# Attention on one core: values times turned probabilities as three products of rounded parts, copied out of PSUM by two engines

## The chip, the cores and the metric

The kernel runs on 1 core of one Trainium2 chip. The metric is the device time of one execution in microseconds. The core has five engines that work beside each other: TensorE (PE in the profile, PEld for its weight loads), VectorE (DVE), ScalarE (ACT), GpSimd (POOL) and SyncE (SP, which starts the DMAs). They order their work by semaphores alone, and each takes its own instructions strictly in order. TensorE's results lie in PSUM, in banks of 512 float32 columns.

## The reference

One step of a two-layer backbone over 640 tokens of width 1024: 512 latent tokens and 128 context tokens. Layer 0 mixes tokens by attention, layer 1 by pooling; behind each comes a mixture of experts with product keys, which takes most of the time. The change lies in the attention:

```python
def block_attention(q, k, v):
    ...
    def one(qi):
        sc = jnp.einsum('bqkgd,btkd->bkgqt', qi, k).astype(jnp.float32) * scale
        p = jax.nn.softmax(sc, axis=-1).astype(v.dtype)
        return jnp.einsum('bkgqt,btkd->bqkgd', p, v)
```

There are 8 query heads and 2 key/value heads of 128. A latent query sees 640 keys (128 cached and 512 of its own), a context query the 128 context keys. All is float32.

## The kernel before

The work of all engines around the attention follows one list, `order_of_units` (L100). It is written out by hand, and TensorE (L1675) and ScalarE (L854) both walk it; VectorE's order is written out separately (`attention`, L1049). A unit of the list has a name and a class, and the class fixes the PSUM tensor: scores go to `bankA` in turns, turned probabilities to `bankD[0]` (class T), the products with the values and some modulation products to `bankD[1]` (class M). Each of these tensors spans two banks.

The stage has 8 heads with 5 tiles of 128 queries, so 40 scores, numbered n = 5 x head + tile. Tiles 0 to 3 are latent (640 keys), tile 4 is context (128 keys). For each n the list says: score n, for n mod 5 = 4 in the first six heads a modulation product (`ada`), for n mod 5 = 0 behind those heads its turned form (`adat`), for n mod 5 = 2 from n = 7 on the values product (`pv`) of the head before, and then the transposes (`pt`) of n-2.

- TensorE: `score` (L1771 to L1783) two matmuls of 512 and 128 columns, `pt` (L1784 to L1789) five transposes of 128x128, side by side in `bankD[0]`, columns 0 to 640; `pv` (L1790 to L1798) five float32 matmuls with 512 columns, the values `vA` against the turned probabilities `PT`, and one with 128 columns for the context tile. A float32 matmul has two records in the trace.
- ScalarE, in the list's order: the exponential of score n with its sum (L945; it waits for VectorE's maximum and for the transposes of n-2, L887 to L890), the copies of `ada` (L894) and `adat` (L897), and for `pv` the copy of the output (L948) and its rounding to float32r (L950). Behind head 6 it also rounds two blocks of the output weights (L951 to L954, through L837).
- VectorE, for each n (L1126 to L1134): `row_max(n)` (L1104, L1105), `normalise(n-1)` (L1111, L1112), `keep_transposed(n-2)` (L1115 to L1124), which copies `bankD[0]` to `PT` and frees the bank, and for n mod 5 = 4 from head 1 on the low part of the head before (`head_rest`, L1035).

`prob` has two buffers, `PT` two (L319, in the place of `sq`), `bankD[0]` one. Behind the stage stands the output projection `wo` (L1799 to L1816), which works with rounded parts already: a high part, rounded to float32r, and a low part, the rest, and three products of them (high x high, high x low, low x high). The expert stage does the same (L1594 to L1608). The parts of the normed input, `hhi` and `hlo`, serve the projections ahead of the stage only, and the last rows of `headr`/`headw` the rotary.

Of the kernel before, what the change touches and what calls it, by code (L numbers as in the profile page):

```python
# [18 lines left out]
ALU = mybir.AluOpType  # L19
# [5 lines left out]
P = 128  # L25
# [7 lines left out]
NH, NKV, HD = 8, 2, 128  # L33
KT = (P + TS) // P
SCALE = HD ** -0.5
EPS = 1e-6
# [159 lines left out]
def build(nc, ins, outs):  # L196
# [47 lines left out]
    with ExitStack() as ctx:  # L244
# [24 lines left out]
        gate = sb("gate", [P, NG])  # L269
        aval = sb("aval", [P, NG])  # L270
        actg = sb("actg", [P, NG])
# [9 lines left out]
        with ExitStack() as front:  # L281
# [36 lines left out]
            ow_split = [split_pair(headr, b) for b in range(2)]  # L318
            PT = sq[:, :, :].rearrange("p k t -> p (k t)").rearrange("p (b j q) -> p b j q", b=2, j=KT)  # L319
            with ExitStack() as rt:  # L320
# [88 lines left out]
        ohi_ready = sem("ohi_ready")  # L409
        olo_ready = sem("olo_ready")  # L410
        sq_ready = sem("sq_ready")
        scaled = sem("scaled")
# [305 lines left out]
        def _(act):  # L718
# [135 lines left out]
            for name, cls in ORDER:  # L854
# [4 lines left out]
                if kind == "wo" and name[1] < K - 2:  # L859
                    act.wait_ge(d_full, Dn[name] + 1)  # L860
                    split_weight(NSPLIT + name[1] + 2)
                if cls not in ("A", "M"):
                    continue
# [78 lines left out]
                elif kind == "score":  # L942
                    b = name[1] % 2
                    w = KT * P if name[1] % TILES < TILES - 1 else P
                    act.activation(prob[:, b, 0:w], bank[:, 0:w], ACT.Exp, bias=smx[:, b, 1:2],  # L945
                                   scale=of_unit(rq, name[1]), accum_out=smx[:, b, 2:3]).then_inc(a_free, 1)
                elif kind == "pv":
                    act.copy(OT[:, name[1], :], bank[:, 0:T]).then_inc(m_free, 1)  # L948
                    act.wait_ge(m_free, n + 1)
                    act.copy(ohi[:, name[1], :], OT[:, name[1], :]).then_inc(ohi_ready, 1)  # L950
                    if name[1] == NH - 2:  # L951
                        act.wait_ge(rope_done, NH + NKV)
                        split_weight(NSPLIT)
                        split_weight(NSPLIT + 1)  # L954

        @block.vector
        def _(v):
# [91 lines left out]
            def attention():  # L1049
# [65 lines left out]
                def keep_transposed(n):  # L1115
# [4 lines left out]
                    if t < TILES - 1:  # L1120
                        v.tensor_copy(PT[:, h % 2, :, t * P:(t + 1) * P],
                                      bankD[0][:, 0:KT * P].rearrange("p (j q) -> p j q", q=P)).then_inc(t_free, 1)
                    else:
                        v.tensor_copy(PTp[:, h % 2, :], bankD[0][:, 0:P]).then_inc(t_free, 1)  # L1124

                for n in range(NH * TILES + 2):  # L1126
                    if n < NH * TILES:
                        row_max(n)
                    if 1 <= n <= NH * TILES:
                        normalise(n - 1)  # L1130
# [328 lines left out]
        def _(pe):  # L1459
# [215 lines left out]
            for name, cls in ORDER:  # L1675
# [108 lines left out]
                elif kind == "pt":  # L1784
# [3 lines left out]
                    for j in range(KT if name[1] % TILES < TILES - 1 else 1):  # L1788
                        last = pe.transpose(bank[:, j * P:(j + 1) * P], prob[:, name[1] % 2, j * P:(j + 1) * P], ident)  # L1789
                elif kind == "pv":  # L1790
                    h = name[1]
                    kv = h // (NH // NKV)
                    pe.wait_ge(t_free, Tn[("pt", h * TILES + TILES - 1)] + 1)
                    pe.wait_ge(a_free, A[("v", TILES - 1)] + 1)
                    for j in range(KT):
                        pe.matmul(bank[:, 0:TS], vA[:, j, kv * HD:(kv + 1) * HD], PT[:, h % 2, j, :],
                                  start=j == 0, stop=j == KT - 1)
                    last = pe.matmul(bank[:, TS:T], vP[:, kv * HD:(kv + 1) * HD], PTp[:, h % 2, :], start=True, stop=True)  # L1798
# [114 lines left out]
```

## Time and profile before

| | |
|---|---|
| three runs, median | 3225.47 us (3223.08 to 3232.5) |
| the profiled execution, its span from the first to the last instruction | 3225.0 us |
| mean granted TensorE clock in it | 0.985 |
| busy: TensorE, VectorE, GpSimd, ScalarE | 3107.2, 2872.3, 1999.2, 1110.5 us |

For the profiled execution its span is the one time that is given. Busy times are sums over instructions; matmuls are pipelined and their ends modelled, so that records overlap and a busy TensorE is not one at its peak. The row of an instruction has its start, its length and, in brackets, how long its engine had stood idle before it and what ended that. "issue" is a wait that the profile can't name.

### The profile page before, as it was taken

What the parts mean: (1) busy time and instruction counts of PE and PEld (TensorE: products, weight loads), DVE (VectorE), ACT (ScalarE), POOL (GpSimd) and SP (SyncE); (2) the same over time, 40 slices, a digit from 0 to 9 for tenths busy, and PEclk for the clock granted to TensorE, in tenths of its full rate; (3) what the DMA queues carried; (4) which work ended last, traced back from release to release, by engine and by line L of the source; (5) the groups of instructions that cost most, each with busy time, mean ns of one, the idle gap of its engine ahead of it and who ended that gap; (6) DMA issues with size and microseconds to landing.
All of it is one profiled execution on the core that took longest, in us unless ns stands there. A gap on an engine that the chain in (4) does not pass through costs nothing.

```text
span 3225.0 us, 50321 instructions
## 1 busy us (share of the span) xinstructions
PE 3107.2 (96%) x15946; PEld 2595.0 (80%) x15946; DVE 2872.3 (89%) x5518; ACT 1110.5 (34%) x1693; POOL 1999.2 (62%) x1483
## 2 busy tenths in 40 slices
PE   7998999989999999999997999979999999999998
PEld 6857566669999999999986466669999999999997
DVE  3574699999999999999998699999999999999998
ACT  3332333333333333333333233333333333333333
POOL 1000166677778887777773067767777877777773
PEclk9999999999999999999998999989999999999999
DMA  5230456689999999999997354589999999999995
GB/s 241 78 135 28 157 215 254 256 346 409 408 408 399 407 399 389 410 408 401 376 406 283 151 196 195 222 314 409 405 409 401 403 404 387 410 408 404 401 400 226
DMA packets 248396, 1044.93 MB, mean 324 GB/s; under 512 B 23024, under 2 KB 72944, under 8 KB 205808
## 3 DMA queue, kind: packets, MB, share of 16 engines
q0 software_dynamic: 147456, 536.94, 42.2%
q1 hardware_dynamic: 100848, 506.86, 39.8%
q8 instruction: 47, 0.77, 0.1%
q14 instruction: 45, 0.37, 0.0%
HBM read 990.49 MB, written 53.22 MB: 324 GB/s over the span
## 4 chain that ended last, share of the span: by engine, by line
PE 77%; DVE 11%; issue 5%; DMA 4%; POOL 1%; ACT 1%; DVEq 1%; POOLq 0%; SPq 0%; ACTq 0%
PE bankA L1594 10%; PE bankA L1596 10%; PE bankA L1595 10%; PE bankD L1607 6%; PE bankD L1608 6%; PE bankD L1606 6%; PE bankA L1548 5%; PE bankA L1608 3%; PE bankA L1607 3%; PE bankA L1606 3%; PE bankD L1516 2%; DMA hT<-in_v,idxc 2%; DVE wch L1370 2%; DMA wch<-in_wq 2%; DVE hot L1320 2%
## 5 line engine op out<-in xcount | busy, mean ns | idle before, releaser
L1594 PE MATMUL bankA<-hh,uh 128*128 128x384 f32 x2048 | 689.4, 337 | 25.6 <-DVE ul L1354 25.6
L1596 PE MATMUL bankA<-hh,ul 128*128 128x384 f32 x2048 | 689.3, 337 | 0.0
L1595 PE MATMUL bankA<-hl,uh 128*128 128x384 f32 x2048 | 687.8, 336 | 0.0
L681 POOL DMA_INDIRECT hT<-in_v,idxc x320 | 469.2, 1466 | 161.5 <-issue 72.2
L681 POOL DMA_INDIRECT hT<-in_u,idxc x320 | 466.5, 1458 | 164.8 <-issue 75.4
L807 ACT ACTIVATE wt<-bankA 128x384 f32<-128x384 f32 x256 | 126.0, 492 | 1120.5 <-PE bankA L1596 881.7
L1594 PEld LDWEIGHTS bankA<-hh,uh 128*128 128x128 f32 x2048 | 386.2, 189 | 37.4 <-issue 26.6
L1370 DVE SCALAR_TENSOR_TENSOR wch<-hT,a,wch 128x1024 f32<-128x1024 f32 x320 | 399.5, 1280 | 10.6 <-DMA hT<-in_v,idxc 6.4
L1607 PE MATMUL bankD<-vl,wh 128*128 128x512 f32 x1024 | 399.9, 390 | 0.0
L1608 PE MATMUL bankD<-vh,wl 128*128 128x512 f32 x1024 | 399.4, 390 | 0.0
L1606 PE MATMUL bankD<-vh,wh 128*128 128x512 f32 x1024 | 398.3, 389 | 0.0
L1595 PEld LDWEIGHTS bankA<-hl,uh 128*128 128x128 f32 x2048 | 386.1, 189 | 9.8
L1361 DVE CUSTOM_DVE_ANT_0 hT<-hT,htok 128x1024 f32<-128x1024 f32 x320 | 382.6, 1221 | 11.7 <-DMA hT<-in_u,idxc 9.4
L647 POOL TENSOR_TENSOR mask<-mask,topf 128x1024 f32<-128x1024 f32 x36 | 84.1, 2358 | 494.9 <-DVE mask L1281 494.9
L1596 PEld LDWEIGHTS bankA<-hh,ul 128*128 128x128 f32 x2048 | 385.7, 188 | 0.0
L1382 DVE TENSOR_TENSOR vl<-vraw,vh 128x1024 fp32r<-128x1024 f32 x256 | 312.7, 1221 | 27.0 <-ACT vh L811 23.7
L681 POOL DMA_INDIRECT wch<-in_u,idxc x192 | 293.7, 1530 | 59.6 <-issue 59.6
L1354 DVE TENSOR_TENSOR ul<-uraw,uh 128x1024 fp32r<-128x1024 f32 x256 | 312.2, 1220 | 0.3
L1548 PE MATMUL bankA<-wch,hT 128*128 128x512 f32 x640 | 289.5, 595 | 3.3 <-DMA wch<-in_wq 1.9
L681 POOL DMA_INDIRECT wch<-in_v,idxc x192 | 232.1, 1209 | 63.3 <-issue 60.5
L797 ACT CAST uh<-uraw 128x1024 fp32r<-128x1024 f32 x256 | 268.8, 1051 | 0.0
L811 ACT CAST vh<-vraw 128x1024 fp32r<-128x1024 f32 x256 | 266.4, 1041 | 0.0
(244 smaller groups left out, 5632.9 us busy)
## 6 DMA issues: line engine op xcount, KB each, us to landing
uraw<-in_uT SPq DMA_DIRECT2D x128, 1024.0 KB
vraw<-in_vP SPq DMA_DIRECT2D x128, 1024.0 KB
wch<-in_wq SPq DMA_DIRECT2D x32, 2048.0 KB, 7.6
gates_scratch<-gbuf SPq DMA_DIRECT2D x12, 4096.0 KB, 11.8
wch<-gates_scratch SPq DMA_DIRECT2D x64, 768.0 KB
wch<-in_ada SPq DMA_DIRECT2D x19, 2048.0 KB, 7.5
wch<-in_qkv SPq DMA_DIRECT2D x3, 2048.0 KB, 23.9
adap<-in_ada SPq DMA_DIRECT2D x3, 2048.0 KB, 17.3
```

The source lines that it names most:

```text
L681: pool.indirect_dma_start(out=row_buf[slot], out_offset=None, in_=table.rearrange("l e d -> (l e) d"), in_offset=bass.IndirectOffsetOnAxis ...
L1354: v.tensor_tensor(ul[:, c, :], uraw[:, b, c * D:(c + 1) * D], uh[:, c, :].bitcast(F32), ALU.subtract).then_inc(ul_ready, 1)
L1361: v.tensor_tensor_reduce(out=row_buf[r % RING], in0=row_buf[r % RING], in1=htok[:, r % GT, :], scale=1.0, scalar=0.0, op0=ALU.mult, op1=AL ...
L1370: v.scalar_tensor_tensor(out=acc[:, r % GT, :], in0=row_buf[r % RING], scalar=a8[:, r:r + 1], in1=acc[:, r % GT, :], op0=ALU.mult, op1=ALU ...
L1382: v.tensor_tensor(vl[:, c % 2, :], vraw[:, b, c % 2 * D:(c % 2 + 1) * D], vh[:, c % 2, :].bitcast(F32), ALU.subtract).then_inc(vl_ready, 1)
L1548: last = pe.matmul(bank, hT[:, k, t * P:(t + 1) * P], w[:, k, :], start=k == 0, stop=k == K - 1)
L1594: pe.matmul(abank[c], hi, hh[:, k, :], start=k == 0, stop=False)
L1595: pe.matmul(abank[c], hi, hl[:, k, :], start=False, stop=False)
L1596: last = pe.matmul(abank[c], lo, hh[:, k, :], start=False, stop=k == K - 1)
L1606: pe.matmul(y, hi, vh[:, c, a:a + 512], start=first, stop=False)
L1607: pe.matmul(y, hi, vl[:, c, a:a + 512], start=False, stop=False)
L1608: last = pe.matmul(y, lo, vh[:, c, a:a + 512], start=False, stop=final)
```

## The change

The turned probabilities and the values are each split in a high part (rounded to float32r) and a low part, and the values product becomes three float32r products for each of the five key tiles: 15 matmuls with 512 columns in place of five float32 ones. ScalarE writes the high part of the turned probabilities from PSUM, VectorE subtracts it from PSUM to get the low part. The five transposes now go to columns 0 to 384 (one bank) and 512 to 768 (the other), and each bank has a copy and a subtraction of its own. The high parts of the values are written once by ScalarE ahead of the first exponential, the low parts by VectorE in step n = 2. The parts lie in tensors that are unused in this stage (`hhi`, `hlo`, the end of `headr`), and the last low part of the values takes the place of `aval`, which serves later.

```diff
+PTCUT = ((0, 3), (3, KT))
...
-        aval = sb("aval", [P, NG])
+        with ExitStack() as plain:
+            aval = sb("aval", [P, NG], where=plain)
+        vlast = sb("vlast", [P, NKV * HD], F32R)
...
-            PT = sq[:, :, :].rearrange("p k t -> p (k t)").rearrange("p (b j q) -> p b j q", b=2, j=KT)
+            parts_of = lambda x: x[:, :, :].rearrange("p k t -> p (k t)").rearrange("p (b j q) -> p b j q", b=2, j=KT)
+            PTh, PTl = parts_of(hhi), parts_of(hlo)
+            v0 = headr[:, 10 * T - (2 * KT - 1) * NKV * HD:10 * T].rearrange("p (j n) -> p j n", n=NKV * HD)
+            vhi, vlo = v0[:, 0:KT, :], v0[:, KT:2 * KT - 1, :]
...
+                if cls == "T" and name[1] % TILES < TILES - 1:
+                    h, t = divmod(name[1], TILES)
+                    if t == 0 and h >= 2:
+                        act.wait_ge(m_full, Mn[("pv", h - 2)] + 1)
+                    act.wait_ge(t_full, Tn[name] + 1)
+                    for i, (j0, j1) in enumerate(PTCUT):
+                        act.copy(PTh[:, h % 2, j0:j1, t * P:(t + 1) * P],
+                                 bankD[0][:, i * 512:i * 512 + (j1 - j0) * P].rearrange("p (j q) -> p j q", q=P)).then_inc(pth_ready, 1)
...
+                    if name[1] == 0:
+                        act.wait_ge(att_in, 48)
+                        act.wait_ge(a_free, A[("v", TILES - 1)] + 1)
+                        act.copy(vhi, vA[:, :, :]).then_inc(vhi_ready, 1)
                     act.activation(prob[:, b, 0:w], bank[:, 0:w], ACT.Exp, bias=smx[:, b, 1:2],
...
-                        v.tensor_copy(PT[:, h % 2, :, t * P:(t + 1) * P],
-                                      bankD[0][:, 0:KT * P].rearrange("p (j q) -> p j q", q=P)).then_inc(t_free, 1)
+                        for i, (j0, j1) in enumerate(PTCUT):
+                            v.wait_ge(pth_ready, (h * (TILES - 1) + t) * 2 + i + 1)
+                            some = PTh[:, h % 2, j0:j1, t * P:(t + 1) * P].bitcast(F32)
+                            last = v.tensor_tensor(PTl[:, h % 2, j0:j1, t * P:(t + 1) * P],
+                                                   bankD[0][:, i * 512:i * 512 + (j1 - j0) * P].rearrange("p (j q) -> p j q", q=P),
+                                                   some, ALU.subtract)
+                        last.then_inc(t_free, 1)
...
+                    if n == 2:
+                        v.wait_ge(vhi_ready, 1)
+                        v.tensor_tensor(vlo, vA[:, 0:KT - 1, :], vhi[:, 0:KT - 1, :].bitcast(F32), ALU.subtract)
+                        v.tensor_tensor(vlast[:, :], vA[:, KT - 1, :], vhi[:, KT - 1, :].bitcast(F32), ALU.subtract
+                                        ).then_inc(vlo_ready, 1)
...
-                        last = pe.transpose(bank[:, j * P:(j + 1) * P], prob[:, name[1] % 2, j * P:(j + 1) * P], ident)
+                        o = j * P if j < PTCUT[0][1] else 512 + (j - PTCUT[0][1]) * P
+                        last = pe.transpose(bank[:, o:o + P], prob[:, name[1] % 2, j * P:(j + 1) * P], ident)
...
+                    pe.wait_ge(vlo_ready, 1)
                     for j in range(KT):
-                        pe.matmul(bank[:, 0:TS], vA[:, j, kv * HD:(kv + 1) * HD], PT[:, h % 2, j, :],
-                                  start=j == 0, stop=j == KT - 1)
+                        cols = slice(kv * HD, (kv + 1) * HD)
+                        pe.matmul(bank[:, 0:TS], vhi[:, j, cols], PTh[:, h % 2, j, :], start=j == 0, stop=False)
+                        pe.matmul(bank[:, 0:TS], vhi[:, j, cols], PTl[:, h % 2, j, :], start=False, stop=False)
+                        rest = vlo[:, j, cols] if j < KT - 1 else vlast[:, cols]
+                        pe.matmul(bank[:, 0:TS], rest, PTh[:, h % 2, j, :], start=False, stop=j == KT - 1)
```

## Rows read from the trace of the kernel before

**Rows 1.** The page, busy time and its share of the span, by engine.

```profile
PE 3107.2 (96%) x15946; PEld 2595.0 (80%) x15946; DVE 2872.3 (89%) x5518; ACT 1110.5 (34%) x1693; POOL 1999.2 (62%) x1483
```

**Rows 2.** The table of stretches: stretch, length, busy time of each engine, granted clock.

```profile
144.40:279.55 135.15, 118.67 (x556) 67.68 (x556) 93.19 (x216) 50.60 (x110) 0.00 (x0) 0.96 0.27 103
```

**Rows 3.** The timeline of one head, VectorE (DVE), ScalarE (ACT): start us, length us, engine, line.

```profile
193.54 0.81 DVE L1104 TENSOR_REDUCE smx<-bankA 128x1 f32<-128x640 f32 x1
...
199.13 0.82 DVE L1121 COPY sq<-bankD 128x640 f32<-128x640 f32 x1 [3.86 <-PE bankD L1789]
...
199.99 0.68 ACT L948 COPY qT<-bankD 128x640 f32<-128x640 f32 x1
...
200.21 0.83 DVE L1104 TENSOR_REDUCE smx<-bankA 128x1 f32<-128x640 f32 x1 [0.26 <-PE bankA L1781]
...
200.70 0.73 ACT L950 CAST qTr<-qT 128x640 fp32r<-128x640 f32 x1
...
201.33 0.88 ACT L945 ACTIVATE prob<-bankA,smx,rq 128x640 f32<-128x640 f32 x1
...
202.59 0.28 DVE L1104 TENSOR_REDUCE smx<-bankA 128x1 f32<-128x128 f32 x1
...
203.63 0.46 ACT L945 ACTIVATE prob<-bankA,smx,rq 128x128 f32<-128x128 f32 x1 [1.33 <-DVE smx L1105]
...
204.08 0.57 ACT L894 COPY adar<-bankD 128x512 f32<-128x512 f32 x1
...
204.43 0.82 DVE L1035 TENSOR_TENSOR qTr<-qT,qTr 128x640 fp32r<-128x640 f32 x1
...
205.16 0.82 DVE L1104 TENSOR_REDUCE smx<-bankA 128x1 f32<-128x640 f32 x1
...
207.35 0.15 ACT L897 COPY mod<-bankD 128x8 f32<-128x8 f32 x1
...
207.57 0.82 DVE L1104 TENSOR_REDUCE smx<-bankA 128x1 f32<-128x640 f32 x1 [0.21 <-PE bankA L1781]
...
208.68 0.89 ACT L945 ACTIVATE prob<-bankA,smx,rq 128x640 f32<-128x640 f32 x1 [1.18 <-DVE smx L1105]
...
209.42 0.82 DVE L1104 TENSOR_REDUCE smx<-bankA 128x1 f32<-128x640 f32 x1
```

**Rows 4.** The same timeline, TensorE.

```profile
193.72 4.53 PE L1796 MATMUL bankD<-sq,vA 128*128 128x512 f32 x10 [0.76 <-issue]
...
198.31 0.71 PE L1789 MATMUL bankD<-const,prob 128*128 128x128 f32 x5
```

**Rows 5.** The timeline of the expert stage, TensorE.

```profile
1500.02 0.39 PE L1607 MATMUL bankD<-vl,wh 128*128 128x512 f32 x1
...
1500.70 0.39 PE L1607 MATMUL bankD<-vl,wh 128*128 128x512 f32 x1
```

**Rows 6.** Groups by line: duration ns min/median/max, first and last start us.

```profile
L1074 DVE TENSOR_TENSOR ropes<-bankD,trig x10: 684/692/693, 82.5 to 143.5; 128x512 f32<-128x512 f32 x10
...
L837 ACT CAST headr<-wch x8: 1040/1048/1049, 264.5 to 321.8; 128x1024 fp32r<-128x1024 f32 x8
```

**Rows 7.** The timeline, ScalarE ahead of the first exponential.

```profile
145.82 1.28 ACT L945 ACT_TABLE_LOAD   x1 [0.95 <-PE bankA L1781]
```

**Rows 8.** The timeline around three rests, and the clock of one microsecond.

```profile
250.37 0.77 PE L1789 MATMUL bankD<-const,prob 128*128 128x128 f32 x5 [1.73 <-DVE sq L1121]
...
256.93 4.53 PE L1796 MATMUL bankD<-sq,vA 128*128 128x512 f32 x10 [0.47 <-issue]
...
265.93 0.77 PE L1789 MATMUL bankD<-const,prob 128*128 128x128 f32 x5 [1.73 <-DVE sq L1121]
...
268.97 1.33 PE L1789 MATMUL bankD<-const,prob 128*128 128x128 f32 x5 [2.27 <-DVE sq L1121]
...
272.12 7.20 PE L1796 MATMUL bankD<-sq,vA 128*128 128x512 f32 x10 [0.43 <-issue]
...
267.00:268.00 1.00, 0.00 (x0) 0.63 0.00 0
```

More of the change, by code:

```diff
@@ L410, in build @@
         olo_ready = sem("olo_ready")
+        vhi_ready = sem("vhi_ready")
+        vlo_ready = sem("vlo_ready")
+        pth_ready = sem("pth_ready")
         sq_ready = sem("sq_ready")
```

## The prediction

> **What bounds the kernel now.** I read the page's busy line first: TensorE is busy 96% of the span, VectorE 89%, ScalarE 34% [rows 1]. That is an average over stages, and the edit touches one of them only: from 144.4 to 279.6 us, between the rotary and the output projection. The table of stretches gives that stage 135.15 us, with TensorE busy 118.7, VectorE 93.2 and ScalarE 50.6, so nobody is full [rows 2]. Everything behind the stage waits for it (the output projection needs the last head), and its loads wait for uses, so a delay here should pass to the end one for one.
>
> The order in time says what the limit is. The stage repeats once per head, 40 units in all, five to a head. I number them by n mod 5: units 0 to 3 are wide (640 keys), unit 4 is narrow (128). From one head's row maximum of unit 2 (193.54) to the next head's (209.42) 15.88 us pass [rows 3]. In it TensorE runs ten records for the values product, 4.5 us in one piece, and the next transposes start 4.59 us after it [rows 4]; meanwhile VectorE waits 3.86 us for those transposes, and so does ScalarE. In the rest of the head VectorE works without a stop: the starts of its row maxima follow each other by 2.38, 2.57, 2.41 and 1.85 us, and the fifth step, across the product, takes 6.67 [rows 3]. So the stage is bound by a loop: VectorE's chain in four steps, TensorE's product in the fifth. ScalarE has slack, but in a fixed order.
>
> **The change, part by part.** One rule of reading: an instruction on VectorE or ScalarE lets the next one start about 0.1 us before its own recorded end (204.43 + 0.82 against 205.16) [rows 3].
>
> *The product.* Of the 4.59 us [rows 4] the narrow context product and the first transpose take 0.32, leaving ten fp32 records 0.427 us apart, 4.27 us. They become 15 products of rounded parts. In the expert stage such products with 512 columns start 0.228 us apart (1500.02 to 1500.70, three steps) [rows 5]. 15 x 0.228 = 3.42 us, so 0.85 us less per head, on the path of the fifth step. The Trainium skill (TensorE: Matmul & The Clock Gate, Back-to-back issue gap) gives about 131 ns per matmul of 512 columns for a sustained stream. By it the product would take an estimated 1.97 us, the gain would be 2.3 us per head, and the sum below an estimated 12 us smaller. This case's dense stream shows 0.228, which decides.
>
> *VectorE's work.* The 640-column copy (0.82) becomes two subtractions, of 384 and 256 columns. A subtraction or multiplication from PSUM costs 0.69 for 512 columns and 0.82 for 640 [rows 3, 6], 1.0 ns a column: 0.56 and 0.43, and 0.46 + 0.33 to the next start, against 0.73 for the copy. Only 0.06 us more. The work isn't the price.
>
> *The wait that is added.* The subtraction waits for ScalarE's rounded copy of the same bank, and in ScalarE's queue this copy stands behind the exponential of unit n, which itself waits for VectorE's row maximum n, and behind whatever comes between: the copy of the modulation product, of its turned form, or the two passes over the product's output. VectorE can then start no row maximum until it is through. ScalarE's copies: 0.57 for 512, 0.68 for 640 [rows 3], so 0.46 for 384 and 0.35 for 256. Let a be the start of the first copy: first subtraction at a + 0.50, second at a + 0.96 (its copy was ready at about a + 0.75, so the second bank's copy is hidden), VectorE free at a + 1.29, bank free at a + 1.39. Now the five steps, from row maximum to row maximum:
> - wide units without extra work (3 to 4): maximum and its scaling until the exponential 1.11 (207.57 to 208.68), exponential 0.88, then 1.29: 3.28 (before 2.38).
> - 4 to 0: the transposes of unit 2 start only when the bank is free, 0.10 after the maximum's start, and take 0.77 and two handovers, so the narrow exponential begins at 0.95; then 0.45, the modulation copy 0.50, 1.29, and the head's rest 0.73: 3.92 (before 2.57).
> - 0 to 1: 1.11 + 0.88 + 0.17 + 1.29 = 3.45 (before 2.41).
> - 1 to 2: narrow, no copy by ScalarE: 1.85 as before.
> - 2 to 3: product 3.42 and the 0.32 behind it, transposes 0.82 (198.31 to 199.13) [rows 3, 4], exponential 0.88, output copy 0.71 and rounding 0.63, 1.29, and 0.18 by which the maximum precedes the product: 8.25 (before 6.67). The shorter product is in it; the copy behind 2.2 us of ScalarE work more than eats it.
>
> Sum 20.75 us, 4.87 more than 15.88.
>
> *The first head.* The rounding of the values (1280 columns) stands ahead of the first exponential. ScalarE's rounding of 1024 takes 1.05 [rows 6], so 1.25. The table load (1.28), hidden today in front of that exponential [rows 7], may now follow the rounding: bounds 0 and 1.28, I take it whole, since the load's own row names the exponential's line and not the copies'. That makes 2.5 for the start of the chain. VectorE's two subtractions of the values in front of unit 1's division: 1.13 + 0.33, near 1.5, by 1.0 ns a column. By row maximum 3 the two make 4.2 later (a few tenths of the 1.5 lie beside ScalarE's work). The steps 3 to 4, 4 to 0 (here with no head's rest) and 0 to 1 add 0.9, 0.7 and 0.7: 6.5 us before the first product.
>
> *The last two heads.* The seventh has no modulation copies: 4.6. In the eighth ScalarE does two weight roundings (1.99) before it would reach the copy: the chain of that head, laid out like the one above, comes to 19.2 us, 4.0 more than the 15.19 of before (256.93 to 272.12) [rows 8]. The last product runs mostly at half clock today, 7.2 us [rows 8]; 15 products, 12 or 13 at 0.43 and the rest at 0.228, give 6.1: 1.0 less.
>
> At full clock: 6.5 + 5 x 4.87 + 4.6 + 4.0 - 1.0 = 38.5 us.
>
> *The clock.* TensorE's granted clock averages 0.96 over the stage [rows 2]. The loss lies at its end: the clock goes from 1.0 (2.4 GHz) to 0.5 (1.2 GHz) within the microsecond from 267, and most of the last product still runs at 0.5, 7.2 us against 4.53 [rows 4, 8]. Around the fall the engine rested 1.73 and then 2.27 us with 0.77 us of transposes between. A rest of 1.73 us at 248.64, between full stretches, cost nothing [rows 8]. The schedule above gives each head one rest of 2.55 us (from the scores of unit 3 until the bank is free) and one of 2.3 us (after the scores of unit 1). Those lie between the two cases. The unknown's ends: 0 if none makes the clock fall; at the other end two falls a head, each costing about half the TensorE work of some 4 us on the path, 2 us, 8 x 4 = 32. I take a fall in about half of the heads at 2 us, 8 us, as by length these rests are nearer to the second of the pair that fell than to the one that held.
>
> Sum: 38.5 + 8 = 46.5. The profiled span is 3225.0 us; nothing lies beside it in the figures, and the median of the three runs is 3225.47, so they stand alike. **Forecast 3272 us.**
>
> **The rivals.**
> (a) *The clock holds.* For it: a single rest of 2.3 or 2.55 us is shorter than the two together that stand around today's fall. Against: it is longer than the one that held. 3225.5 + 38.5 = 3264.
> (b) *The clock falls twice in each head.* Then 38.5 + 32: 3296. Against it: the products and the scores behind them are 5.6 us without a gap, which lifts it.
> (c) *The other side: the copy is hidden.* The place is ScalarE's queue, where the rounded copy of unit n-2 stands behind the exponential of unit n. It decides from the point where that copy is through before VectorE has divided unit n-1, 1.65 us after its row maximum (2.38 less the copy's 0.73). Then the steps stay as they are, VectorE pays 32 x 0.06 = 1.9 us and the start some 4, and the product gives back 7 x 0.85 + 1.0 = 7.0: 3224, no change. It speaks for it that ScalarE is busy only 37% of the stage (50.6 of 135.15) [rows 2]. Against: the exponential can't begin before 1.11 and takes 0.88, so the copy starts at 1.99 at the earliest. Only an overestimate of this order by me would bring it.
> (d) *The product costs as much in rounded parts as in fp32*, because its operands come from other tiles: the 15 take the 4.27 us of today, nothing is gained, 3279. The stream of the expert stage speaks against it.
> (e) *The product's matmuls follow more closely than the expert stage's.* Two of each three here use the same weights; if the second of them cost half of 0.228, a head saves 5 x 0.114 more, eight heads 4.6: 3267. No row shows such a step. The figure in the Trainium skill's page on TensorE named above would give an estimated 3260.
>
> **How the numbers follow.** Forecast with clock falls in some heads 0.57, (a) 0.22, (b) 0.05, (c) 0.08, (d) 0.05, (e) 0.03. A measurement of this kernel can tell about 0.3%, 9.7 us, from no change. Only (c) ends within it, and a part of (c), with a cheap start and a product gaining more than it does here, could be faster: 0.03 faster, 0.05 same, 0.92 slower. The range runs from 3253 (case (a) with the table load hidden, 1.3, and each of 40 steps 0.25 us cheaper) to 3290 (two falls in three of the heads and one in each of the others, 22 us in place of 8, and a first head dearer by 4).
>
> **What would show it.** VectorE's second kind of work in the stage at 0.56 and 0.43 us, 32 of each; its idle time ahead of the first one released by ScalarE, near 0.8 us in a plain wide unit and 2 us more after the product; ScalarE's copies at 0.46 and 0.35; 15 product matmuls within 3.4 us; product to product 20.7 us instead of 15.9; the stage some 45 us longer, and the later stages as long as before. I am wrong if VectorE finds its copy ready, if TensorE is the last to arrive in the plain units, or if the granted clock sits at 0.5 through much of the stage.

## The result, and the profile after

The changed kernel takes 3275.4 us (median of 4 runs, 3274.5 to 3280.1) against 3224.6 before: ratio 1.0152, 95% interval 1.014 to 1.0164. It is slower by 51 us. The forecast was 3272, and 3275 lies in its range (3253 to 3290). One run of experiment 3 took 3478.2 us at a granted clock of 0.841; without it the median there is 3223.0 and not 3223.8.

The profiled execution took 3280.1 us, its span is 3278.3. The page's busy line answers to [rows 1]:

```profile
PE 3125.4 (95%) x15986; PEld 2617.8 (80%) x15986; DVE 2876.9 (88%) x5552; ACT 1133.7 (35%) x1758; POOL 1967.9 (60%) x1483
```

Busy times move little beside 53 us: VectorE has 5 us more, TensorE 18, ScalarE 23. The attention stage, from the first score matmul to the output projection, answers to [rows 2] (stretch, length, busy time of TensorE, weight loads, VectorE, ScalarE and GpSimd, granted clock, DMA share and GB/s):

```profile
145.39:333.68 188.29, 131.99 (x595) 85.45 (x594) 97.31 (x250) 73.45 (x175) 0.00 (x0) 0.85 0.20 74
```

It grew from 134.9 us (144.41 to 279.3) to 188.3, by 53.4; the whole span grew by 53.3. What comes behind the stage takes 2944.6 us against 2945.7, and what comes ahead 1 us more. So the time went into this stage alone. In it VectorE is busy for 4 us more, ScalarE for 23 and TensorE for 13 (its matmuls are longer where the clock is low), all well under 53: what grew is idle time. The list of waits of the stage (engine and line that waited, on whom, us in total, times, the longest) names it:

```profile
DVE hlo L1145 <- ACT hhi L877: 78.0, 31, 7.8
```

VectorE waits 78 us in 31 of its 32 low parts for ScalarE's rounded copy. Before, it waited 27.5 us for TensorE at this place:

```profile
DVE sq L1121 <- PE bankD L1789: 27.5, 9, 3.9
```

The timeline of one head (VectorE and ScalarE; start us, length, engine, line, operation, idle time before and what ended it) answers to [rows 3]:

```profile
197.06 0.88 ACT L966 ACTIVATE prob<-bankA,smx,rq 128x640 f32<-128x640 f32 x1 [4.54 <-issue]
...
197.94 0.68 ACT L969 COPY qT<-bankD 128x640 f32<-128x640 f32 x1
198.65 0.72 ACT L971 CAST qTr<-qT 128x640 fp32r<-128x640 f32 x1
199.28 0.75 ACT L877 CAST hhi<-bankD 128x384 fp32r<-128x384 f32 x2
199.88 0.89 DVE L1145 TENSOR_TENSOR hlo<-bankD,hhi 128x384 fp32r<-128x384 f32 x2 [5.88 <-ACT hhi L877]
200.69 0.81 DVE L1125 TENSOR_REDUCE smx<-bankA 128x1 f32<-128x640 f32 x1
...
202.24 0.89 ACT L966 ACTIVATE prob<-bankA,smx,rq 128x640 f32<-128x640 f32 x1 [2.21 <-DVE smx L1126]
...
203.12 0.74 ACT L877 CAST hhi<-bankD 128x384 fp32r<-128x384 f32 x2
203.69 0.89 DVE L1145 TENSOR_TENSOR hlo<-bankD,hhi 128x384 fp32r<-128x384 f32 x2 [1.28 <-ACT hhi L877]
204.50 0.28 DVE L1125 TENSOR_REDUCE smx<-bankA 128x1 f32<-128x128 f32 x1
```

This is the circle of the prediction: ScalarE's exponential (202.24) waits for VectorE's maximum, its copy (203.12) stands behind the exponential, VectorE's subtraction waits for the copy, and the next maximum (204.50) stands behind the subtraction. After the product ScalarE first does the exponential and two passes over the output (197.06 to 199.28) before it comes to the copy.

The same head also shows the clock. TensorE, and then the granted clock (stretch, length, TensorE's busy time, clock, DMA share and GB/s):

```profile
200.83 1.32 PE L1821 MATMUL bankD<-const,prob 128*128 128x128 f32 x5 [2.77 <-DVE hlo L1145]
...
202.51 3.64 PE L1730 MATMUL bankD<-wch,cs 128*32 128x512 f32 x16
```

```profile
198.00:201.00 3.00, 0.23 (x2) 0.85 0.00 0
201.00:204.00 3.00, 3.00 (x15) 0.50 0.00 0
204.00:207.00 3.00, 3.00 (x17) 0.52 0.00 0
207.00:210.00 3.00, 2.57 (x16) 1.00 0.96 317
```

The clock falls to 0.5 (1.2 GHz) in a rest of 2.77 us and stays there for nearly 7 us. Read in stretches of half a microsecond, the table shows ten times of low clock in the stage, most of them 3.5 to 4 us long and the last, from 316 to 333.5, through the eighth head and its product; before there was one (267 to 277.5). The modulation product takes 3.64 us where it takes 1.92 at full clock in the first head. The transposes behind it start 1.58 us after the row maximum, against 0.14 in the first head.

The steps between row maxima (differences of their starts), by unit as in the prediction; "full clock" is read from the heads in which no fall lies in the step:

| step | before | forecast | after, full clock | after, with a fall |
|---|---|---|---|---|
| 3 to 4 | 2.38 | 3.28 | 3.35 | 3.6, 3.8 |
| 4 to 0 | 2.57 | 3.92 | 4.04 | 4.85 to 5.86 |
| 0 to 1 | 2.41 | 3.45 | 3.42 | |
| 1 to 2 | 1.85 | 1.85 | 1.84 | 2.86 |
| 2 to 3 | 6.67 | 8.25 | 8.21 to 8.41 | 9.94, 9.96 |

The heads, from product to product, take 22.1, 23.7, 21.5, 23.6, 23.7, 21.1 and 21.2 us, where they took 15.2 to 15.9.

### The profile page after: what moved, and what is told of

It reads as the page before. It is cut to its first block, busy times and chain, and to the rows that moved or that the text cites. A ratio compares the mean times of both kernels' runs of the same rounds, so it can differ in the third digit from the quotient of the medians.

```text
span 3278.3 us, 50541 instructions
## 1 busy us (share of the span) xinstructions
PE 3125.4 (95%) x15986; PEld 2617.8 (80%) x15986; DVE 2876.9 (88%) x5552; ACT 1133.7 (35%) x1758; POOL 1967.9 (60%) x1483
## 4 chain that ended last, share of the span: by engine, by line
PE 78%; DVE 7%; issue 3%; DMA 1%; POOL 1%; DVEq 0%; ACT 0%; POOLq 0%
PE bankA L1625 11%; PE bankA L1627 11%; PE bankA L1626 11%; PE bankD L1638 7%; PE bankD L1639 7%; PE bankD L1637 7%; PE bankA L1579 6%; PE bankA L1639 4%; PE bankA L1638 4%; PE bankA L1637 4%; PE bankD L1547 2%; DVE hot L1351 1%; PE bankD L1846 1%; PE bankA L1533 1%; DMA wch<-in_wq 1%
## 5 line engine op out<-in xcount | busy, mean ns | idle before, releaser
L1625 PE MATMUL bankA<-hh,uh 128*128 128x384 f32 x2048 | 688.5, 336 | 21.5 <-DVE ul L1385 21.5
L690 POOL DMA_INDIRECT hT<-in_v,idxc x320 | 454.9, 1421 | 173.9 <-issue 68.2
```

Source lines behind the costliest of these rows:

```text
L690: pool.indirect_dma_start(out=row_buf[slot], out_offset=None, in_=table.rearrange("l e d -> (l e) d"), in_offset=bass.IndirectOffsetOnAxis ...
L1625: pe.matmul(abank[c], hi, hh[:, k, :], start=k == 0, stop=False)
```

## The experiments

Each is the changed kernel with one edit, unless it says otherwise. "Stage" is from the first row maximum to the output projection in the profiled run (133.0 before, 186.4 changed), "time" the median. The kernel before gave 3225.2, 3224.9, 3225.4 and 3227.6 us beside the four groups of runs.

**1. The copy ahead of the exponential.**

```diff
+                if kind == "score" and name[1] >= 2 and (name[1] - 2) % TILES < TILES - 1:
+                    high_probs(name[1] - 2)
                 if kind == "score":
                     act.wait_ge(negmax_ready, name[1] + 1)
...
-                if cls == "T" and name[1] % TILES < TILES - 1:
+                if cls == "T" and name[1] % TILES < TILES - 1 and name[1] + 2 >= NH * TILES:
+                    high_probs(name[1])
```

> The changed kernel, with one thing moved: ScalarE's two rounded copies of the turned tile n-2 stand ahead of its exponential n instead of behind it; same instructions. Theory 1 (the price is the place of the copy in ScalarE's queue): the copy runs beside VectorE's row maximum, VectorE finds it ready in the plain steps, the steps go back to 2.4 to 2.5 us (3 to 4: about 3.0, as ScalarE is then still busy with the head's output), across the product about 6.0, a head about 16.0 us in place of 21 to 23.7; time about 3232 to 3236. Theory 2 (the price is the work itself: more instructions on VectorE and ScalarE): under 5 us fall, 3270 or more.

Time 3236.7 (ratio 1.0033, 1.002 to 1.0045), stage 143.5. With the same instructions 39 of the 51 us are gone, 0.7 us short of the range of theory 1 (3232 to 3236). The steps are 2.84, 3.06, 2.71, 1.84 and 6.2 us, a head 16.64: theory 1, theory 2 is out. The timeline shows what is left:

```profile
224.47 0.74 ACT L868 CAST hhi<-bankD 128x384 fp32r<-128x384 f32 x2
225.04 0.89 DVE L1151 TENSOR_TENSOR hlo<-bankD,hhi 128x384 fp32r<-128x384 f32 x2 [0.31 <-ACT hhi L868]
225.10 0.90 ACT L972 ACTIVATE prob<-bankA,smx,rq 128x640 f32<-128x640 f32 x1
225.85 0.28 DVE L1131 TENSOR_REDUCE smx<-bankA 128x1 f32<-128x128 f32 x1
```

VectorE still waits 0.3 to 0.45 us a tile, and no longer for a copy that stands behind an exponential: the loop is now bank free, transposes, copy, subtraction. I had expected 16.0 us a head; 0.6 of that loop I had not seen. Of the ten times of low clock only two are left (151 to 154.5 and 277 to 287.5), so the 39 us hold what those falls cost as well; experiment 5 prices them apart. The waits of the stage, beside the 78.0 us of the changed kernel:

```profile
DVE hlo L1151 <- ACT hhi L868: 37.6, 29, 3.7
```

**2. VectorE without the wait.** The low parts of the probabilities are left out; VectorE does two subtractions of the same size on keys in SBUF, and TensorE waits for ScalarE before it writes the bank again.

```diff
-                            v.wait_ge(pth_ready, (h * (TILES - 1) + t) * 2 + i + 1)
-                            some = PTh[:, h % 2, j0:j1, t * P:(t + 1) * P].bitcast(F32)
                             last = v.tensor_tensor(PTl[:, h % 2, j0:j1, t * P:(t + 1) * P],
-                                                   bankD[0][:, i * 512:i * 512 + (j1 - j0) * P].rearrange("p (j q) -> p j q", q=P),
-                                                   some, ALU.subtract)
+                                                   kA[:, 0, j0 * P:j1 * P].rearrange("p (j q) -> p j q", q=P),
+                                                   kA[:, 1, j0 * P:j1 * P].rearrange("p (j q) -> p j q", q=P), ALU.subtract)
...
+                    if name[1] and (name[1] - 1) % TILES < TILES - 1:
+                        h, t = divmod(name[1] - 1, TILES)
+                        pe.wait_ge(pth_ready, (h * (TILES - 1) + t) * 2 + 2)
```

> The changed kernel, but VectorE's two subtractions take their operands from the keys in SBUF, so that they wait for the transposes alone and not for ScalarE; TensorE waits for ScalarE's copies before it writes the bank again. Left out: the true low parts of the probabilities. Theory 1 (VectorE's strict order turns ScalarE's lateness into a stop of the row maxima): plain steps near 2.5 us, across the product near 5.5 and the step behind it near 3.9, a head near 16.6 us; time 3234 to 3242. Theory 2 (what costs is that the one bank of turned tiles comes free later, whoever waits): it comes free as late as before, steps of 3.3 stay, 3265 or more.

Time 3245.4 (1.0058, 1.0042 to 1.0075): 30 us fall off with VectorE's stop alone, in the direction of theory 1 and 3 us above its range. Plain steps are 2.44; across the product 5.5 as expected, behind it 3.6 (I had expected 3.9), but the step 4 to 0 takes 3.5 where the 16.6 us of the expectation leave 2.8, 1 to 2 takes 2.22, and two heads hold a fall of the clock (18.9 in place of 17.3). So part of theory 2 holds as well: the steps 3 to 4, 4 to 0 and 1 to 2 are together 2.5 us longer than before, and TensorE's transposes now wait for ScalarE's copy, longest behind the product, where ScalarE is late by its output passes:

```profile
210.25 0.73 PE L1822 MATMUL bankD<-const,prob 128*128 128x128 f32 x5 [2.12 <-ACT hhi L877]
```

**3. The product alone.** Before's single copy by VectorE, rounded, and three products that all take this one part; the low parts of the probabilities are left out.

```diff
-                    for i, (j0, j1) in enumerate(PTCUT):
-                        act.copy(PTh[:, h % 2, j0:j1, t * P:(t + 1) * P],
...
-                        for i, (j0, j1) in enumerate(PTCUT):
-                            v.wait_ge(pth_ready, (h * (TILES - 1) + t) * 2 + i + 1)
...
+                        v.tensor_copy(PTh[:, h % 2, :, t * P:(t + 1) * P],
+                                      bankD[0][:, 0:KT * P].rearrange("p (j q) -> p j q", q=P)).then_inc(t_free, 1)
...
-                        pe.matmul(bank[:, 0:TS], vhi[:, j, cols], PTl[:, h % 2, j, :], start=False, stop=False)
+                        pe.matmul(bank[:, 0:TS], vhi[:, j, cols], PTh[:, h % 2, j, :], start=False, stop=False)
```

> The kernel before with the product of 15 rounded matmuls and with the split of the values at the start, but the turned probabilities are written once, by VectorE, rounded, as one copy of 640 columns; all three products take this one part. Left out: the low parts of the probabilities. Both theories: 0.85 us less in each head and 0.75 less in the last product, 7 us less; the start, 7.4 us dearer in the changed kernel, stays dearer by some 4 to 7 (the clock may fall there): time 3222 to 3228. If the rounded product costs as much as the float32 one in this stage, it is 3230 or more.

Time 3223.8 (0.9997, 0.9987 to 1.0007), as expected. A head takes 15.09 us against 15.88, so the rounded product gives 0.79 us a head, not 0.85; the other four steps are those of before. The start takes 4.6 us more than before (20.35 against 15.71 from first maximum to first product) and eats the larger part of it: the stage is 130.1 us, 2.9 less than before, and the medians don't tell it from no change.

**4. The values later.** ScalarE rounds them behind the exponential of tile 1, GpSimd makes the low part.

```diff
-                    if name[1] == 0:
+                    act.activation(prob[:, b, 0:w], bank[:, 0:w], ACT.Exp, bias=smx[:, b, 1:2],
+                                   scale=of_unit(rq, name[1]), accum_out=smx[:, b, 2:3]).then_inc(a_free, 1)
+                    if name[1] == 1:
                         act.wait_ge(att_in, 48)
                         act.wait_ge(a_free, A[("v", TILES - 1)] + 1)
                         act.copy(vhi, vA[:, :, :]).then_inc(vhi_ready, 1)
...
+            pool.wait_ge(vhi_ready, 1)
+            pool.tensor_tensor(vlo, vA[:, 0:KT - 1, :], vhi[:, 0:KT - 1, :].bitcast(F32), ALU.subtract)
+            pool.tensor_tensor(vlast[:, :], vA[:, KT - 1, :], vhi[:, KT - 1, :].bitcast(F32), ALU.subtract
+                               ).then_inc(vlo_ready, 1)
```

> The changed kernel, but ScalarE rounds the values behind the exponential of tile 1 instead of ahead of that of tile 0, and GpSimd, idle here, makes their low part instead of VectorE. Theory 1 (the first head's term is the rounding and the table load behind it, 2.5 us, and VectorE's 1.5): the first product comes 4 to 5 us earlier, the table load is hidden again; time 3270 to 3272. Rival (the start is hidden behind other waits, the 7.4 us come from the steps of the first head alone): under 2 us, 3274 or more.

Time 3276.7 (1.0166, 1.0149 to 1.0183): no gain that can be told; a miss. The profiled run has its first product at 20.84 us behind the first maximum, 2.2 us earlier where I had expected 4 to 5, and the table load is hidden again. But VectorE's division of tile 1 took 2.22 us where all others of its size take 0.55 (experiment 10 takes that up), and the clock still fell near the start. The profiled stage is 2.7 us shorter (183.7), the medians show none of it. That the clock falls hide it (the runs scatter from 3274.1 to 3283.0) is likely and not shown.

**5. TensorE kept at work in its rests.**

```diff
+                if kind == "score" and name[1] > TILES and name[1] % TILES in (1, 3):
+                    pe.wait_ge(a_free, n)
+                    for i in range(1 if name[1] % TILES == 1 else 2):
+                        pe.matmul(bankA[(n + 1) % 2][:, 0:512], ident, const[:, 0:512], start=True, stop=True)
```

> The changed kernel, with TensorE kept at work in its two rests of each head from tile 8 on: two float32 matmuls of 512 columns (0.85 us each) behind the scores of unit 3, one behind those of unit 1, into the score tensor that is free then; their output is overwritten. Theory 1 (some 8 to 12 us of the loss are falls of the granted clock in these rests): the clock stays at 1.0 from the second head to the last product, the steps 4 to 0 go to 4.0 everywhere and those across the product to 8.4; time 3262 to 3268. Rival (low clock lies beside VectorE's and ScalarE's chain and costs next to nothing): clock up, time within 2 us of the changed kernel, 3273 to 3277.

Time 3269.2 (1.0137, 1.012 to 1.0154), 6 us below the changed kernel, though above the range by 1; the runs of the two lie apart (3267.0 to 3271.6 and 3274.5 to 3280.1), while the intervals of their ratios overlap. The stretch from the first product to the last, in the changed kernel and in this one (length, TensorE's busy time, clock, DMA):

```profile
170.35:327.28 156.93, 109.55 (x500) 0.86 0.18 69
```

```profile
169.00:316.00 147.00, 115.60 (x541) 0.96 0.20 74
```

With more matmuls the stretch is 10 us shorter, the clock at 0.96 in place of 0.86, and five heads in a row take 21.01 to 21.06 us, all at the steps of the column "full clock". Of the ten times of low clock two are left, one ahead of the first product and one from 304.5 on, so "1.0 to the last product" was too much said. The other eight cost 10 us in the profiled run, 1.2 us each, and 6 in the medians.

**6. Both parts on VectorE.**

```diff
-                    for i, (j0, j1) in enumerate(PTCUT):
-                        act.copy(PTh[:, h % 2, j0:j1, t * P:(t + 1) * P],
...
+                        turned_p = bankD[0][:, 0:KT * P].rearrange("p (j q) -> p j q", q=P)
+                        some = PTh[:, h % 2, :, t * P:(t + 1) * P]
+                        then(v.tensor_copy(some, turned_p))
+                        v.tensor_tensor(PTl[:, h % 2, :, t * P:(t + 1) * P], turned_p, some.bitcast(F32), ALU.subtract
+                                        ).then_inc(t_free, 1)
```

> The changed kernel, but VectorE writes the high part too, as one copy of 640 columns, and then subtracts in one piece; ScalarE writes nothing of it. So VectorE has 0.8 us more work for each wide tile and no wait for ScalarE. Theory 1 (the wait costs more than the work): plain steps 3.15 to 3.2 us in place of 3.35, 4 to 0 3.4 in place of 4.0 to 5.9, across the product 6.3 in place of 8.4; a head near 17.9; time 3244 to 3250. Theory 2 (work on VectorE is the bound): slower than the changed kernel, above 3278.

Time 3245.7 (1.0065, 1.0048 to 1.0081), a head 17.87, steps 3.23, 3.43, 2.97, 1.84 and 6.4. With more work on the engine that is busiest of the two, and none shared, the kernel is 30 us faster than with the work divided in the order of the change. It is slower than experiment 1, where the division stands in the right order.

**7. and 8. The two moves together, and the output of a head one unit later.** In 8 the passes over the output (L948, L950) wait in ScalarE's order until the exponential of unit 3; for the seventh head the two weight roundings go with them.

```diff
+                    if kept and name[1] % TILES == 3:
+                        keep_head(kept.pop())
```

> The two moves together: ScalarE's rounded copies ahead of the exponential, and the values rounded behind the exponential of tile 1 with their low part made by GpSimd. If the two terms add: 4 to 5 us below the run with the copies moved alone, 3228 to 3231. If they overlap (the start is then bound by something else): as that run.

> As the run before, and ScalarE copies out and rounds a head's output behind the exponential of unit 3 instead of unit 2. By the schedule the step 3 to 4 then falls from 3.0 to 2.5, 0.5 us a head, 3 to 4 us in all: 3225 to 3228, level with the kernel before. If it is slower than the run before, what waits is the modulation product, whose bank the output holds longer.

7 gave 3236.6 (1.0037, 1.0023 to 1.0051), the time of experiment 1: the moves don't add, though the first product comes 1.5 us earlier behind the first maximum. Of these, 0.7 go again in the last product, which takes 6.0 us in place of 5.3, most of it at half clock. 8 gave 3253.5 (1.0088, 1.0071 to 1.0105), 17 us worse. The step 3 to 4 did fall to 2.44, and 4 to 0 rose from 3.06 to 7.18:

```profile
237.54 0.70 ACT L881 COPY qT<-bankD 128x640 f32<-128x640 f32 x1
...
238.29 3.06 PE L1748 MATMUL bankD<-wch,cs 128*32 128x512 f32 x16 [2.08 <-ACT qT L881]
241.28 1.27 PE L1839 MATMUL bankD<-const,prob 128*128 128x128 f32 x5
```

TensorE's modulation product waits for the bank that holds the output, runs mostly at half clock after that rest (3.06 us; the clock is low from 239 to 242.5), and the transposes stand behind it: the same pattern again, a wait in a strict order that holds up what is queued behind. It is the case that the expectation had named.

**9. and 12. Two products.** As 3, without the middle product (the edit is against the kernel of experiment 3): rounded probabilities against the high and the low part of the values. The low parts of the probabilities are left out. In 12 ScalarE rounds the values behind the exponential of tile 2 and VectorE makes their low part at n = 5.

```diff
-                        pe.matmul(bank[:, 0:TS], vhi[:, j, cols], PTh[:, h % 2, j, :], start=False, stop=False)
```

> As the run of the product alone, with two products instead of three for each key tile: the rounded probabilities against the high and the low part of the values; 10 matmuls a head. Left out: the low parts of the probabilities, and nothing else. If the stage is bound across the product by its matmuls, a head falls by another 5 x 0.228 = 1.14 us to 13.95, 9 us in all: 3213 to 3217, below the kernel before. If something else is last there by now (ScalarE's exponential, VectorE's maximum), less than half of that: 3219 or more.

> As the run with two products, but ScalarE rounds the values behind the exponential of tile 2 and VectorE makes their low part in step n = 5, where it waited in the kernel before. Left out: the low parts of the probabilities. The first product came 20.6 us after the first row maximum with two products, 15.7 in the kernel before; if the rounding and the table load behind it (2.5 us) and the clock fall they bring are the cause, it comes at 17 to 17.5, and the time falls by some 3.5 us to 3212 to 3215. If the start's delay is taken up elsewhere: as the run before, 3216 to 3218.

9 gave 3216.7 (0.9973, 0.9962 to 0.9984), a head 13.92, 1.17 less than in 3, and all of it in the step across the product (4.71 against 5.87): there the stage is still bound by the matmuls. 12 gave 3211.2 (0.9952, 0.9938 to 0.9965), the fastest of all: the first product at 16.44 us behind the first maximum in place of 20.55. That is earlier than I expected (17 to 17.5): the time of low clock near the start (151.5 to 155.5 in 9) is gone, and VectorE's two subtractions, 1.5 us by themselves, lengthen their step by 0.8 only (3.59 against 2.83), as VectorE waited in it before. Both beat the kernel before. They round the probabilities and don't make that good; whether this accuracy is enough is a question of use, not one of time.

**10. The values' low part on VectorE.** As 7, with VectorE in GpSimd's place.

> As the run with both moves, but VectorE makes the values' low part, GpSimd nothing. Theory (in that run VectorE's division of tile 1 took 2.2 us in place of 0.55 because GpSimd's subtraction ran beside it): the division is back at 0.55, VectorE pays 1.5 us itself instead; first product up to 1 us earlier or later, time 3233 to 3237, the same. If the division stays at 2.2 us, GpSimd had nothing to do with it, and the time is 1.5 us more.

Time 3235.1 (1.0028, 1.0018 to 1.0039). VectorE and GpSimd in run 7, then VectorE in run 10:

```profile
152.65 2.21 DVE L1143 TENSOR_SCALAR prob<-prob,smx 128x640 f32<-128x640 f32 x1
154.78 0.88 DVE L1155 TENSOR_TENSOR hlo<-bankD,hhi 128x384 fp32r<-128x384 f32 x2
```

```profile
152.17 2.34 POOL L644 TENSOR_TENSOR headr<-vA,headr 128x1024 fp32r<-128x1024 f32 x1 [92.17 <-ACT headr L977]
154.47 0.97 POOL L645 TENSOR_TENSOR vlast<-vA,headr 128x256 fp32r<-128x256 f32 x1
```

```profile
151.72 0.55 DVE L1138 TENSOR_SCALAR prob<-prob,smx 128x640 f32<-128x640 f32 x1
```

The division ends 0.35 us after GpSimd's first subtraction (154.86 and 154.51) and takes 0.55 where GpSimd rests. Work given to an idle GpSimd was paid by VectorE, here 1.7 us, as much as VectorE's own two subtractions take in 10 (1.5).

**11. One piece instead of two banks.**

```diff
-                    for i, (j0, j1) in enumerate(PTCUT):
+                    for i, (j0, j1) in enumerate(((0, KT),)):
```

(in both engines, and the transposes side by side again)

> The changed kernel, but the five transposes stand side by side again, ScalarE copies all 640 columns at once and VectorE subtracts them at once, so that the two engines don't work on two banks at the same time. By the schedule the copy takes 0.68 before VectorE may start, and VectorE 0.73: 1.45 against 1.29, 0.16 us more for each of 32 wide tiles: 5 us, 3279 to 3282. If the split in two banks hides more than that (0.4 us a tile, as if the second copy were hidden whole): 3287. If it hides nothing: 3275.

Time 3285.9 (1.0185, 1.0172 to 1.0199), between two of the ranges. The plain step is 3.50 in place of 3.35, 0 to 1 3.57 in place of 3.42: 0.15 us a tile, the schedule's figure. That is half of the 10 us between the medians, and nearly all of what the profiled runs differ by (stage 191.0 against 186.4). The other half is in no trace. The profiled run has twelve times of low clock in place of ten (3.95 and 4.25 in steps 3 to 4, five steps across the product above 9.6), and the granted clock of its runs is 0.975 to 0.978 where the changed kernel's later three have 0.978, so more falls are the likely cause, not a shown one. The cut in two banks is worth 10 us in the changed order, 5 of them by the overlap.

## Why the prediction was right

- *What bounds the stage*, VectorE's chain in four steps and the product in the fifth: held; experiments 3 and 9 move only the fifth step, by 0.79 and 1.96 us.
- *The product*, 0.85 us a head: measured 0.79. The 15 matmuls start 0.232 us apart here (306.36 to 309.38, 13 steps), not 0.228, and the first takes 0.3. Rival (d) and (e) are out: neither the old price nor a closer rhythm.

```profile
306.36 0.39 PE L1831 MATMUL bankD<-hlo,headr 128*128 128x512 f32 x1
...
309.38 0.40 PE L1833 MATMUL bankD<-hhi,vlast 128*128 128x512 f32 x1
```

- *VectorE's work*: the row of its subtractions reads 412 to 559 ns, against 0.43 and 0.56 forecast; ScalarE's copies 372 to 491 ns against 0.35 and 0.46.

```profile
L1145 DVE TENSOR_TENSOR hlo<-bankD,hhi x64: 412/484/559, 157.5 to 325.9; 128x384 fp32r<-128x384 f32 x32, 128x256 fp32r<-128x256 f32 x32
```

```profile
L877 ACT CAST hhi<-bankD x64: 372/430/491, 156.3 to 325.2; 128x384 fp32r<-128x384 f32 x32, 128x256 fp32r<-128x256 f32 x32
```

- *The wait*: the five steps came within 0.01 to 0.16 us each; a head at full clock is 21.05 against 20.75. Experiments 1, 2 and 6 show that the place in the queue is the price. Rival (c), the hidden copy, is what experiment 1 brings about by an edit, and what the change as written excludes. VectorE's idle time ahead of the subtraction is 1.2 to 1.3 us in plain units, where I had named 0.8 as the sign; 0.2 us of it are the wait for TensorE's scores of before, which is in it now.
- *The first head*, 6.5: 7.4 measured. The rounding and the table load came in a row:

```profile
148.39 1.26 ACT L965 CAST headr<-vA 128x1280 fp32r<-128x1280 f32 x1 [2.54 <-DVE smx L1126]
...
149.66 1.28 ACT L966 ACT_TABLE_LOAD   x1
150.96 0.88 ACT L966 ACTIVATE prob<-bankA,smx,rq 128x640 f32<-128x640 f32 x1
```

  Taking the load's upper bound was right. Not foreseen: TensorE rests 4.2 us meanwhile, and the scores of tile 2 run at half clock (1.81 us in place of 1.02). So row maximum 2 comes 3.5 us later and not 2.5, and VectorE's subtractions add the 1.5 of the forecast: 5.0 by row maximum 3. The forecast's 4.2 there is no sum of its parts, which are 2.5 and 1.5 less a few tenths.
- *The last heads*: the seventh 5.5 more than before (4.6), of which 0.6 are a fall of the clock (experiment 5, where it holds there, has 20.5 us for this head, 4.9 more than before); the eighth 6.0 (4.0), the last product 0.8 less (1.0). The eighth head is short by 2. Across the product it takes 10.3 us, as the forecast's steps have it (8.25, and 1.99 for the two weight roundings); the 2 us lie behind that, in the long time of low clock, where three sets of transposes take 1.33 us each in place of 0.77. The forecast's list of rests doesn't have the one ahead of them. No run has this head at full clock, so what the clock costs in it stays open.

```profile
316.30 1.33 PE L1821 MATMUL bankD<-const,prob 128*128 128x128 f32 x5 [4.66 <-DVE hlo L1145]
```

- *At full clock* the sum was 38.5; experiment 5 has 43.3 (stage 176.3 against 133.0), with the eighth head behind its product and most of the last product still at half clock in both.
- *The clock*, 8 us: 10 in the profiled run, 6 between the medians. The size is right by two errors that cancel, so by luck: I had a fall in half of the heads, four, at 2 us each, and besides the two times that experiment 5 leaves there are eight, two in some heads and none in one, at 1.2 us. Why they are cheaper no run shows; part of the low clock may lie beside VectorE's chain. Rival (a), that it holds, is out; rival (b), two falls a head at 2 us, had both the count and the price too high. The rests, 2.77 and 2.31 us, were forecast at 2.55 and 2.3.

The mis-sized term is thus the sum over the heads at full clock, 5 us too low: 0.9 in the first head, 0.3 in each of the five behind it and in the seventh, 2 in the eighth, 0.2 in the last product; it stays inside the range.

## What to carry to other kernels

When work is divided between two engines, look at the queue of the one that helps: an instruction placed behind one which itself waits for the first engine closes a circle, and a share of 0.8 us cost more than the work done alone. Lay out one period by starts, with each instruction in its engine's order, before counting busy time. And when waits open rests on TensorE, the granted clock can take its part on top: 6 to 10 of 51 us here.

## What the runs showed of the hardware that I had not expected

- A VectorE multiplication by a scalar, float32 in SBUF on both sides, 640 columns, took 2.2 us instead of 0.55 while GpSimd subtracted 1024 columns in SBUF, in experiments 4, 7 and 8; it ended 0.35 us after GpSimd's instruction. VectorE's subtraction with one operand in PSUM ran at its usual length (0.88 for two) beside GpSimd's second one. The Trainium skill (SBUF — State Buffer, Terms) says that the two engines share a pair of ports which one holds for a whole instruction, and that the loser blocks; by that rule, the trace agrees.
- ScalarE's and VectorE's passes over PSUM kept their lengths while the other engine read the neighbouring bank. ScalarE's copy of 256 columns takes 0.38 us on average beside VectorE's subtraction from PSUM, and the same in experiment 2, where VectorE reads SBUF; VectorE's subtraction of 384 columns, which runs beside that copy, takes 0.56 us in both.
- With the same schedule in each head the clock falls now behind the one rest and now behind the other. In the seventh head the rest of 2.78 us ended at full clock, and it fell behind the next one, of 2.36 us (changed kernel, TensorE, then two stretches with their clock):

```profile
293.35 0.76 PE L1821 MATMUL bankD<-const,prob 128*128 128x128 f32 x5 [2.78 <-DVE hlo L1145]
...
296.70 1.33 PE L1821 MATMUL bankD<-const,prob 128*128 128x128 f32 x5 [2.36 <-DVE hlo L1145]
```

```profile
290.00:294.00 4.00, 1.22 (x9) 0.85 (x8) 1.60 (x3) 2.51 (x6) 0.00 (x0) 1.00 0.00 0
294.00:297.00 3.00, 0.64 (x6) 0.45 (x5) 2.07 (x8) 1.62 (x4) 0.00 (x0) 0.78 0.00 0
```

  That fall cost 0.6 us, less than the others, in a head without a modulation product: its step 4 to 0 took 4.11 us, and 3.54 in experiment 5, where the same rest of 2.36 us ended at full clock.
